# Stick-breaking attention: the scan's second operand in PSUM, weights rounded and subtracted on GpSimd in three turns of four

## The reference, cut to what matters

```python
def _stick_breaking_attention(q, k, v):
    """A[t,s] = beta[t,s] * prod_{s<j<t} (1 - beta[t,j]), s < t."""
    def block(args):                      # 128 queries at a time, all keys
        z = einsum('bhqd,bhkd->bhqk', qi, k) * inv_sqrt_d
        strict = key_pos[None, :] < q_pos[:, None]
        log_keep = where(strict, log_sigmoid(-z), 0.0)
        after = cumsum(log_keep, reverse=True) - log_keep
        w = where(strict, exp(log_sigmoid(z) + after), 0.0)
        return einsum('bhqk,bhkd->bhqd', w, v)
```

## Time and profile before

| | us |
|---|---|
| median of 3 runs | 2332.32 |
| the profiled execution, its own time | 2329.38 |
| its span | 2327.4 |
| busy in the span: TensorE, VectorE, ScalarE, GpSimd | 1966.4, 1399.7, 941.8, 603.3 |
| `attend_sb`, first matmul to last subtraction | 1004.5 to 1533.8 |

### The profile page before, as it was taken

The page is one execution under the profiler, slowest core; times in us unless marked ns, Lnnn a source line. Parts: engine busy times, 40 slices in busy tenths (PEclk is TensorE's granted clock), DMA queues, the critical chain, the costliest instruction groups (busy, mean ns, idle before and its releaser), DMA issues. The chain is left out here.

```text
span 2327.4 us, 31942 instructions
## 1 busy us (share of the span) xinstructions
PE 1966.4 (84%) x9698; PEld 1574.6 (68%) x9698; DVE 1399.7 (60%) x2006; ACT 941.8 (40%) x1836; POOL 603.3 (26%) x515
## 2 busy tenths in 40 slices
PE   6589999969895577569898888969999999996998
PEld 1368888859784567447676766748777787774777
DVE  2811111121111688669999999969899898984111
ACT  2411111122221333246666666636666666663000
POOL 1400000000000355400000000007777676772222
PEclk9599999979998799879999999969999999997999
DMA  7246544344342366563331614081343440404554
GB/s 283 87 127 181 154 144 131 102 173 147 143 145 111 117 208 208 181 152 73 84 99 45 155 33 113 0 170 48 73 118 73 96 94 28 109 10 154 181 186 157
DMA packets 220290, 284.60 MB, mean 122 GB/s; under 512 B 10736, under 2 KB 158496, under 8 KB 214544
## 3 DMA queue, kind: packets, MB, share of 16 engines
q1 hardware_dynamic: 215344, 270.77, 40.3%
q10 hardware_dynamic: 4832, 12.58, 1.4%
HBM read 164.56 MB, written 114.56 MB: 120 GB/s over the span
## 5 line engine op out<-in xcount | busy, mean ns | idle before, releaser
L1893 POOL TENSOR_TENSOR mla_wl<-mla_w,mla_wh 128x512 fp32r<-128x512 f32 (+1 forms) x280 | 381.4, 1378 | 166.3 <-ACT mla_wh L1930 163.7
L1993 DVE TENSOR_TENSOR mla_acc<-mla_acc,mla_w 128x512 f32<-128x512 f32 (+3 forms) x288 | 271.1, 941 | 40.8 <-ACT mla_w L1928 38.1
L1511 DVE TENSOR_TENSOR_SCAN sb_w<-sb_kp,sb_w 128x512 f32<-128x512 f32 x192 | 245.1, 1277 | 7.3 <-ACT sb_kp L1461 0.9
L1470 ACT ACTIVATE sb_wh<-sb_pt 128x512 fp32r<-128x512 f32 (+1 forms) x320 | 170.5, 533 | 153.7 <-PE sb_pt L1603 146.1
L1928 ACT ACTIVATE mla_w<-mla_zt 128x512 f32<-128x512 f32 (+1 forms) x320 | 170.6, 533 | 144.2 <-PE mla_zt L2080 70.9
L515 PE MATMUL pt_po<-h_hi,pt_wh 128*128 128x512 f32 x512 | 200.3, 391 | 8.0 <-DVE pt_wl L476 8.0
L516 PE MATMUL pt_po<-h_lo,pt_wh 128*128 128x512 f32 x512 | 200.1, 391 | 0.0
L517 PE MATMUL pt_po<-h_hi,pt_wl 128*128 128x512 f32 x512 | 199.9, 390 | 0.0
L1971 DVE TENSOR_REDUCE mla_nmx<-mla_zn 128x1 f32<-128x512 f32 (+2 forms) x320 | 191.5, 600 | 10.3 <-PE mla_zn L2046 7.4
L1461 ACT ACTIVATE sb_kp<-sb_z 128x512 f32<-128x512 f32 (+3 forms) x320 | 169.7, 531 | 52.6 <-PE sb_z L1581 23.1
L1581 PE MATMUL sb_z<-sb_kk,sb_qh 128*128 128x512 f32 (+3 forms) x320 | 146.1, 457 | 37.2 <-DMA sb_ql<-qk_sb 27.7
(11 more groups left out here) (220 smaller groups left out, 4152.6 us busy)
## 6 DMA issues: line engine op xcount, KB each, us to landing
pn_hs<-hT SPq DMA_DIRECT2D x16, 1024.0 KB, 8.4
mod_wada<-in_w_ada SPq DMA_DIRECT2D x6, 2048.0 KB, 7.9
qk_mla<-lat_th SPq DMA_DIRECT2D x32, 384.0 KB, 4.3
qk_mla<-lat_tl SPq DMA_DIRECT2D x32, 384.0 KB, 5.1
mod_x<-in_x ACTq DMA_DIRECT2D x16, 512.0 KB, 4.2
pt_w<-in_w_feat SPq DMA_DIRECT2D x16, 512.0 KB, 6.1
hT<-h_hi SPq DMA_DIRECT2D x16, 512.0 KB, 3.6
hT<-h_lo SPq DMA_DIRECT2D x16, 512.0 KB, 5.2
```

The lines of the kernel that those rows point to most:

```text
L1470: nc.scalar.activation(wh[x % RING][:, lo:GW], pt[x % PTS][:, lo:GW], ACT.Copy, bias=-1.0).then_inc(s_hi if plan.split[x] else s_whole, 1)
L1511: nc.vector.tensor_tensor_scan(kept, keeps, keeps, 1.0 if u["n"] == 0 else w[u["g"]][:, u["r"], b:b + 1], ALU.mult, ALU.bypass).then_inc(s ...
L1893: nc.gpsimd.tensor_tensor(wl[i][:, cols], w[i][:, cols], wh[i][:, cols].bitcast(F32), ALU.subtract).then_inc(s_lo, 1)
L1993: nc.vector.tensor_tensor(a[:, cols], a[:, cols], w[x % RING][:, cols], ALU.add).then_inc(s_acc, 1)
```

## The change

- The scan's second tensor becomes `beside`, a bank of PSUM that VectorE sets to zero once; the transposed banks go from 4 to 3 for it.
- No turn is unsplit. Turns with x mod 4 = 3 are done by ScalarE and VectorE as split turns were before. In the others ScalarE writes the unrounded weights to SBUF (`wf`, three buffers), GpSimd copies them to `wh` (float32r), waits for that copy, and subtracts into `wl`.
- The product runs 3 turns late instead of 2, the groups' ends 4 turns late instead of 3.
- The rounding of the gated output goes from VectorE to ScalarE, one turn after the gate; the subtraction stays on VectorE, two turns after it.

```diff
-    WHOLE = (3,)
+    def pooled(self, x):
+        return x % self.RING != self.RING - 1
-    PTS = 4
+    PTS = 3
...
+        wf = [m.sb(f"wf{i}", [P, GW]) for i in range(RING - 1)]
+        wh = [m.sb(f"wh{i}", [P, GW], F32R) for i in range(RING)]
+        wl = [m.sb(f"wl{i}", [P, GW], F32R) for i in range(RING)]
+        beside = m.ps("beside", [P, GW])
...
-        AFTER = 3
+        AFTER = 4
...
 @block.gpsimd
+            def turn(it, x):
+                if not plan.pooled(x):
+                    return
+                lo, i = plan.turns[x]["lowest"] * P, x % RING
+                pooled = it * plan.pooled_to(T - 1) + plan.pooled_to(x)
+                pool.wait_ge(s_whole, pooled)
+                reached(pool, s_pv, it * T + x + 1 - RING)
+                pool.sem_inc(s_step, 1)
+                nc.gpsimd.tensor_copy(wh[i][:, lo:GW], wf[i][:, lo:GW]).then_inc(s_phi, 1)
+                pool.wait_ge(s_phi, pooled)
+                nc.gpsimd.tensor_tensor(wl[i][:, lo:GW], wf[i][:, lo:GW], wh[i][:, lo:GW].bitcast(F32),
+                                        ALU.subtract).then_inc(s_plo, 1)
...
 @block.scalar
-                reached(act, s_pv, k + 1 - RING)
-                nc.scalar.activation(wh[x % RING][:, lo:GW], pt[x % PTS][:, lo:GW], ACT.Copy,
-                                     bias=-1.0).then_inc(s_hi if plan.split[x] else s_whole, 1)
+                if plan.pooled(x):
+                    reached(act, s_plo, it * plan.pooled_to(T - 1) + plan.pooled_to(x - RING))
+                    nc.scalar.activation(wf[x % RING][:, lo:GW], pt[x % PTS][:, lo:GW], ACT.Copy,
+                                         bias=-1.0).then_inc(s_whole, 1)
+                else:
+                    reached(act, s_pv, k + 1 - RING)
+                    nc.scalar.activation(wh[x % RING][:, lo:GW], pt[x % PTS][:, lo:GW], ACT.Copy,
+                                         bias=-1.0).then_inc(s_hi, 1)
...
+            def high(it, n):
+                act.wait_ge(s_gated, it * EPI2 + k + 1)
+                nc.scalar.activation(mh[b][:], om[:, g * GW:(g + 1) * GW], ACT.Copy).then_inc(s_mh, 1)
...
 @block.vector
+            nc.vector.memset(beside[:], 0.0).then_inc(s_beside, 1)
...
-                nc.vector.tensor_tensor_scan(kept, keeps, keeps,
+                nc.vector.tensor_tensor_scan(kept, keeps, beside[:, 0:b - a],
...
-                if not plan.split[x]:
+                if plan.pooled(x):
                     return
...
 @block.tensor
+            def bank_free(it, x):        # of the turn three before in the same bank
+                if plan.pooled(y):
+                    reached(pe, s_whole, it * plan.pooled_to(T - 1) + plan.pooled_to(y))
+                else:
+                    reached(pe, s_lo, it * plan.others_to(T - 1) + plan.others_to(y))
+            def split(it, x):            # ahead of the product
+                if plan.pooled(x):
+                    reached(pe, s_plo, it * plan.pooled_to(T - 1) + plan.pooled_to(x))
+                else:
+                    reached(pe, s_lo, it * plan.others_to(T - 1) + plan.others_to(x))
...
-                if not plan.split[x]:
-                    nc.tensor.matmul(out, vj.bitcast(F32), wh[x % RING][:, lo:GW], start=tn["first"],
-                                     stop=tn["last"]).then_inc(s_pv, 1)
-                    return
...
-            LAG = 2
+            LAG = 3
```

More of the change, by code:

```diff
@@ L1269, in __init__ @@
                                         units=len(self.units)))
-        self.split = [x % self.RING not in self.WHOLE for x in range(len(self.turns))]
         U, G, T = len(self.units), len(self.groups), len(self.turns)
@@ L1289, in __init__, with pooled_to, others_to, due @@
         self.rest = [(x, 1) for s in self.slots for x, back in s if back]
-    def splits_to(self, x):
-        return sum(self.split[:x + 1])
+    def pooled(self, x):
+        return x % self.RING != self.RING - 1
+    def pooled_to(self, x):
+        return x + 1 - (x + 1) // self.RING
+    def others_to(self, x):
+        return (x + 1) // self.RING
+    def due(self, x, after):
+        ends = [(n, grp["turns"] - 1 + after) for n, grp in enumerate(self.groups)]
+        return [(n, when // self.T) for n, when in ends if when % self.T == x]
     def turns_through(self, group):
@@ L1324, in attend_sb @@
         w = [m.sb(f"w{g}", [P, QG, (g + 1) * GW]) for g in range(GROUPS)]
-        wh = [m.sb(f"wh{i}", [P, GW], F32 if i in plan.WHOLE else F32R) for i in range(RING)]
-        wl = [None if i in plan.WHOLE else m.sb(f"wl{i}", [P, GW], F32R) for i in range(RING)]
+        wf = [m.sb(f"wf{i}", [P, GW]) for i in range(RING - 1)]
+        wh = [m.sb(f"wh{i}", [P, GW], F32R) for i in range(RING)]
+        wl = [m.sb(f"wl{i}", [P, GW], F32R) for i in range(RING)]
         half = m.sb("half", [P, GW])
@@ L1346, in attend_sb @@
         s_t = m.sem("t")
+        s_beside = m.sem("beside")
         s_whole = m.sem("whole")
+        s_phi = m.sem("phi")
+        s_plo = m.sem("plo")
         s_hi = m.sem("hi")
@@ L1359, in attend_sb @@
         EPI2 = G // 2
-        AFTER = 3
-        ends = {plan.groups[n]["turns"] - 1 + AFTER: n for n in range(G - 1)}
+        AFTER = 4
         def pairs(eng, body):
@@ L1447, in _, with body @@
                                     channel_multiplier=-1).then_inc(s_const, 1)
+            def turn(it, x):
[10 more added lines that the diff above has]
+                                        ALU.subtract).then_inc(s_plo, 1)
+            def body(it, start):
+                for x in range(T):
+                    turn(it, x)
+            pairs(pool, body)
         @block.scalar
@@ L1478, in half_sum, with group_ends @@
                 nc.scalar.activation(half[hb:hb + HD, :], po[n % 2][HD:P, :], ACT.Copy).then_inc(s_half, 1)
+            def high(it, n):
+                grp = plan.groups[n]
+                g = grp["g"]
+                if grp["head"] == 0:
+                    return
+                b, k = g % 2, GROUPS - 1 - g
+                act.wait_ge(s_gated, it * EPI2 + k + 1)
+                reached(act, s_st[b], 32 * (it * (EPI2 // 2) + k // 2))
+                nc.scalar.activation(mh[b][:], om[:, g * GW:(g + 1) * GW], ACT.Copy).then_inc(s_mh, 1)
+            def group_ends(it, x):
+                for body, after in ((half_sum, AFTER), (high, AFTER + 1)):
+                    for n, wraps in plan.due(x, after):
+                        if not (isinstance(it, int) and not 0 <= it - wraps < PAIRS):
+                            body(it - wraps, n)
             def slot(it, turns):
@@ L1482, in slot @@
                     turn(it - back, x)
[L1483 to L1486, removed]
+                    group_ends(it - back, x)
             def body(it, start):
@@ L1494, in _ @@
             slot(PAIRS, plan.rest)
-            half_sum(PAIRS - 1, G - 1)
+            for x in range(AFTER + 2):
+                group_ends(PAIRS, x)
         @block.vector
         def _(dve):
+            nc.vector.memset(beside[:], 0.0).then_inc(s_beside, 1)
+            dve.wait_ge(s_beside, 1)
             def unit(it, n):
@@ L1516, in turn @@
                 lo = plan.turns[x]["lowest"] * P
-                if not plan.split[x]:
+                if plan.pooled(x):
                     return
-                dve.wait_ge(s_hi, it * plan.splits_to(T) + plan.splits_to(x))
+                dve.wait_ge(s_hi, it * plan.others_to(T - 1) + plan.others_to(x))
                 nc.vector.scalar_tensor_tensor(out=wl[x % RING][:, lo:GW], in0=pt[x % PTS][:, lo:GW], scalar=-1.0,
@@ L1537, in finish, with low, group_ends @@
                 nc.vector.tensor_tensor(om[:, cols], om[:, cols], gate[b][:], ALU.mult).then_inc(s_gated, 1)
-                dve.wait_ge(s_gated, it * EPI2 + k + 1)
+            def low(it, n):
+                grp = plan.groups[n]
+                g = grp["g"]
+                cols = slice(g * GW, (g + 1) * GW)
+                if grp["head"] == 0:
+                    return
+                b, k = g % 2, GROUPS - 1 - g
                 reached(dve, s_st[b], 32 * (it * (EPI2 // 2) + k // 2))
-                nc.vector.tensor_copy(mh[b][:], om[:, cols]).then_inc(s_mh, 1)
                 dve.wait_ge(s_mh, it * EPI2 + k + 1)
                 nc.vector.tensor_tensor(ml[b][:], om[:, cols], mh[b][:].bitcast(F32), ALU.subtract).then_inc(s_ml, 1)
+            def group_ends(it, x):
+                for body, after in ((finish, AFTER), (low, AFTER + 2)):
+                    for n, wraps in plan.due(x, after):
+                        if not (isinstance(it, int) and not 0 <= it - wraps < PAIRS):
+                            body(it - wraps, n)
             def slot(it, turns):
@@ L1559, in _ @@
             slot(PAIRS, plan.rest)
-            finish(PAIRS - 1, G - 1)
+            for x in range(AFTER + 2):
+                group_ends(PAIRS, x)
         @block.tensor
@@ L1564, in _, with bank_before @@
             pe.wait_ge(s_constr, 2)
```

(15 more changed lines are left out.)

2 lines of the change are left out of this document (1 added, 1 removed).

## The result

| | before | after |
|---|---|---|
| median, us | 2331.24 (2330.05 to 2338.97) | 2304.80 (2301.05 to 2307.50) |
| profiled execution, its span | 2327.4 | 2299.4 |
| `attend_sb`, first matmul to end of last subtraction | 1004.5 to 1533.8 | 1005.2 to 1506.2 |
| mean pair (first to last scores matmul, by four) | 124.9 | 114.9 |
| steady pair (first scan of the second pair to first scan of the fourth, by two) | 130.9 | 120.3 |

The ratio is 0.9885, 95% interval 0.9863 to 0.9907. Forecast were 2300 and a gain. The stage got 28 us shorter, the span 28.0: nothing changed elsewhere. A second set of runs of the changed kernel gave 2303.73 and 0.9872 (0.9842 to 0.9901).

What follows compares the result with a forecast made beforehand. VectorE bounds the kernel before; afterwards GpSimd at 113.5 us a pair: 1030.2 + 4 x 113.5 = 1484, drain to 1489, coupling to 1503 against 1533.8, 31 us off 2329.4, so 2299, forecast 2300; range 2268 to 2350.

Steps and rivals of the forecast that it cites:

- The bound of before: Attention stage before: VectorE's work, start to start, sets the time; modelled 126.7 us a pair against 126.0 measured.
- VectorE after: VectorE in the changed stage: 106.8 us a pair, 110 with 3 us for the shared port.
- The operand and the port: VectorE's scan: one operand in PSUM changes its time by at most 25 ns and avoids taking turns with GpSimd.
- rival four: Shared port: the scan still takes it, scans and GpSimd alternate, 220 us a pair, near 2700; chance 0.03.
- TensorE after: TensorE in the changed stage: 5.6 us a pair less, 97 us a pair, not the bound.
- GpSimd after: GpSimd's 60 turns a pair: 512 copy 0.65 us, 512 turn 2.02, 111.5 us a pair, 113.5 with the port.
- Coupling: New waits between engines in the changed stage: charged 3% of four pairs, 14 us.
- busy over 90%: Sign of the forecast in the profile: GpSimd busy over 90% of this stage from 1030 us on.
- rival three: Engines round the ring: ScalarE and TensorE wait for each other, GpSimd idles 8 to 10%, 2330, no change; chance 0.13.
- ring and lag: Turn's round trip through ScalarE, GpSimd and TensorE: 3.4 us into three slots of about 1.4, fits barely.
- The drain: Stage's end, only turns left: GpSimd keeps its full share, 4.8 us from last weights to last subtraction as before.
- Rival one: GpSimd's copy near the memset, 0.515 to 0.55 us; VectorE bounds at 110 a pair, 2288; chance 0.20.

Runs made afterwards that it cites:

- first experiment: Kernel before with no unsplit turns (WHOLE = ()), nothing else changed: 2367.59 us, ratio 1.0136.
- second: Kernel before with the scan's unused operand in PSUM and three transposed banks, GpSimd idle: 2334.61 us, ratio 0.9991.
- third: Changed kernel with `keeps` given twice to the scan again, so both its inputs are in SBUF: 2496.79 us, ratio 1.069.
- second profile: Profile of the changed kernel unchanged, from its repeat on one chip with two other runs; that repeat measured 2303.73 us, ratio 0.9872.
- fourth: Changed kernel with ScalarE's rounding of the gated output two turns after the gate instead of one, the subtraction three: 2294.21 us, ratio 0.9820.
- eighth experiment: Changed kernel with the rounding one turn later and, in the last pair's last 23 turns, one turn of three on GpSimd: 2281.92 us, ratio 0.9776.
- fifth: Changed kernel with GpSimd's copy cut to the first 128 columns beyond the first turns: 2285.68 us, ratio 0.9791.
- tenth: Changed kernel with the gated output rounded on VectorE, directly ahead of the subtraction, not on ScalarE: 2305.34 us, ratio 0.9873.
- eleventh run: Changed kernel unchanged, run again beside two others on one chip: 2303.73 us, ratio 0.9872.
- ninth: Changed kernel with the product two turns late again (LAG = 2) instead of three: 2352.60 us, ratio 1.0074.
- sixth: Changed kernel with all turns on GpSimd, none on VectorE: 2402.18 us, ratio 1.0296.
- seventh run: Changed kernel with two turns of four on GpSimd (x mod 4 = 0, 2): 2303.55 us, ratio 0.9872.

## Why the prediction was right

- **The bound of before.** Right: first experiment, +32 us for 33 forecast, by VectorE's work alone. The check of the model was looser than it looked: it held the work of four whole pairs, 126.7 each, against the 126.0 up to the drain, though VectorE was busy for another 20 us in the drain. A steady pair took 130.9 us with VectorE busy 126.1, so the model of its work holds, but the kernel before did lose some 2.5 us a pair to waits and 2.3 to VectorE's short gaps. "Lost nothing to coupling" was too much.
- **VectorE after**, 106.8 and 3 for the port, 110 us a pair. Right: in a steady pair it was busy 104.9 us, and the short gaps between its own instructions were another 3.7. The port's share was somewhat smaller than charged (0.32 us on the gate's product, 0.23 on the subtraction, 2 us a pair for 3). The same scans without GpSimd took 1272 ns, with it 1278.
- **The operand and the port.** Right in kind (second and third). The size of rival four, 2700, was too high: 2497.
- **TensorE after**, 97 us a pair by pitches. Not tested: the profile has it busy 110 us of a steady pair, but with modelled ends.
- **GpSimd after.** The copy was 0.61 alone for 0.65 taken, the turn 1.94 for 2.02, so a pair's work about 109 us (44 x 1.94 + 8 x 1.55 + 8 x 1.15, and 2 for the port) for 113.5. The term was 4.5 us a pair too large.
- **Coupling.** Charged with 3%, 14 us. Measured: from its first copy at 1030.9 to the end of its last subtraction at 1501.9 GpSimd took 471 us; it was busy 417, waited for its own copies 240 x 0.08 = 19, and stood idle the remaining 35, 7.4%. In the second profile it was 40 of 476, 8.4%. In a steady pair of 120.3 us it was busy 105.2 and waited for its own copies 4.8, which leaves 10.3 or 8.6%; in the second profile 12.9 of 122.6, 10.5%. So the term was 21 us too small. Of the signs that the prediction gave, "busy over 90%" failed (417 of 471 us, 88.5%), and that of rival three, idle over 8% with waits on ScalarE, stood at the limit over the whole and beyond it in the steady pairs: 31 of its 35 idle us were waits for ScalarE's `sb_wf`. Rival three's mechanism came; its 2330 did not, because GpSimd's own work was 18 us less. I named ring and lag as its place; the largest piece that an experiment could take back, 15 of the 35 us (fourth), was ScalarE's rounding that waits for the gate's product with sigmoids behind it. I had costed that move as a gain on VectorE and as free on ScalarE, and had not asked what stands behind the waiting instruction, nor that the gate's product gets longer. What the prediction said of ring and lag (3.4 us into three slots) held: with two slots 49 us are lost.
- **The drain.** I took it as part of GpSimd's continuous work; it was, and the eighth experiment shows that this part could be had back.

The two terms that were off, 18 us too much on GpSimd's work and 21 too little on coupling, cancel: the stage ended at 1506.2 for 1503 forecast. That they cancel is luck, and so the time of 2304.8 is nearer to 2300 than the working deserves. Rival one needed a cheaper copy, rival two a dearer one, and rival four fell with the scan's 1278 ns.

Not settled is a stall of 2.1 us on ScalarE near the start of a round of its loop (1223.7 to 1225.8), for which the profile shows no wait. It was seen twice in the stage, 4.5 us in all, and after the first GpSimd stood 2.8 us (its copy at 1228.75), so it is a part of the idle time above. Such rows also stand in the fourth, fifth, eighth, tenth and eleventh run, twice each, and in the third and ninth once. None stands in the kernel before or in the first, second, sixth and seventh run. No experiment was made to find its cause.

## What to carry to other kernels

To hand work from a full VectorE to GpSimd, first look at which operations of VectorE have all inputs in SBUF: if an operand is unused by the arithmetic, point it to PSUM, which here cost a bank and nothing else. Then add up both engines' pitches per round, hold them against a steady round and not against a mean with a short first one in it, and leave room for coupling. Here, with three engines near 90% busy, a steady pair took 120.3 us for 110 of work, 9% more, and 6% more with the rounding later. Where an instruction is moved to an engine with room, ask what waits behind it when its input is late; one turn of slack was worth 10 to 15 us, the move by itself nothing. And count the drain by itself: the share that is right beside other work is wrong when that work has ended.

## What the runs showed of the hardware

Undisturbed, GpSimd rounds float32 to float32r, SBUF to SBUF, in 0.61 us for 512 columns, 0.51 for 384 and 0.40 for 256 (changed kernel), and in 0.29 for 128 (fifth and sixth run). That is 0.107 us for 128 columns and 0.18 before the first. At 512 columns it lies between the memset's 0.515 and the 0.876 that the prediction worked out for an affine select; at 128 it equals the affine select's 0.292. The Trainium skill's 1.03 cycles an element ("GPSIMD Engine Reference", the section on elementwise cycle accounting) would be 0.110 us for 128 columns at its 1.2 GHz, an estimate; the trace's slope of 0.107 agrees. Beside scans with both inputs in SBUF the copy of 512 columns took 1.23 us on average (third run).

VectorE's scan of 512 columns took 1277 ns with both inputs in SBUF and GpSimd idle, 1272 with one in PSUM and GpSimd idle, 1278 with one in PSUM beside a busy GpSimd, and 1666 with both in SBUF beside a busy GpSimd.
